# A decoder step on one core: the experts' first gathers and gate splits moved into the attention phase, first rows in halves, a wait moved, and the sample's attention in another order

## The reference, cut to what matters

```python
x = x + MemoryCrossAttn(RMSNorm(x))   # 4 heads over 256 memory tokens
x = x + HierMoE(RMSNorm(x))           # top-1 of 4 groups, then top-2 of 8 experts in it
...
def memory_attn(hn, mem_k, mem_v, w_mq, w_mo):
    q = (hn @ w_mq).reshape(B, T, MEM_HEADS, MEM_DH)
    s = jnp.einsum('bthd,bmhd->bhtm', q, mem_k) * (MEM_DH ** -0.5)
    p = jax.nn.softmax(s, axis=-1)
    return jnp.einsum('bhtm,bmhd->bthd', p, mem_v).reshape(B, T, -1) @ w_mo
...
def expert_block(args):
    xblk, e = args
    h = jax.nn.silu(xblk @ w_e_gate[e]) * (xblk @ w_e_up[e])
    return h @ w_e_down[e]
```

## Time and profile before

| | |
|---|---|
| median of 3 runs | 1961.62 us (1959.93 to 1963.73) |
| profiled execution, its own time | 1965.48 us |
| its span in the trace | 1963.7 us |
| PE busy | 1794.7 us, 91% of the span |
| DVE busy | 1184.4 us, 60% |
| ACT busy | 823.7 us, 42% |
| attention phase ends, experts' phase begins | about 1314.5 us into the span |

### The profile page before, as it was taken

The page is one execution under the profiler, slowest core; times in us unless marked ns, Lnnn a source line. Parts: engine busy times, 40 slices in busy tenths (PEclk is TensorE's granted clock), DMA queues, the critical chain, the costliest instruction groups (busy, mean ns, idle before and its releaser), DMA issues. The chain is left out here.

```text
span 1963.7 us, 35654 instructions
## 1 busy us (share of the span) xinstructions
PE 1794.7 (91%) x14904; PEld 1478.9 (75%) x14904; DVE 1184.4 (60%) x1339; ACT 823.7 (42%) x940; POOL 341.7 (17%) x308
## 2 busy tenths in 40 slices
PE   7999998988888885889999999868999999999995
PEld 6998886777777764678788888647888888878882
DVE  4543111667777665641433433368898898898885
ACT  5111211333343321520212121127777777778763
POOL 1322001233344322000000000011111111111105
PEclk9999998899999987899999999878999999999997
DMA  7756335023222204755200101959999999999988
GB/s 290 243 180 204 115 96 180 13 75 110 97 85 75 85 15 129 258 207 202 97 33 33 65 33 43 371 207 355 403 404 402 404 403 401 403 402 400 405 331 284
DMA packets 113062, 419.13 MB, mean 213 GB/s; under 512 B 26852, under 2 KB 45352, under 8 KB 84008
## 3 DMA queue, kind: packets, MB, share of 16 engines
q1 hardware_dynamic: 100680, 373.76, 51.2%
q0 software_dynamic: 7072, 25.69, 3.5%
q10 hardware_dynamic: 5184, 17.82, 2.2%
HBM read 350.26 MB, written 75.36 MB: 217 GB/s over the span
## 5 line engine op out<-in xcount | busy, mean ns | idle before, releaser
L2715 DVE TENSOR_TENSOR ex_wd_lo<-ex_raw,ex_wd_hi 128x2048 fp32r<-128x2048 f32 x62 | 141.8, 2289 | 50.6 <-ACT ex_wd_hi L2889 50.6
L2715 DVE TENSOR_TENSOR ex_wg_lo<-ex_raw,ex_wg_hi 128x2048 fp32r<-128x2048 f32 x66 | 148.4, 2286 | 10.7 <-ACT ex_wg_hi L2889 10.7
L2715 DVE TENSOR_TENSOR ex_wu_lo<-ex_raw,ex_wu_hi 128x2048 fp32r<-128x2048 f32 x64 | 143.7, 2284 | 0.7 <-ACT ex_wu_hi L2889 0.6
L2889 ACT CAST ex_wg_hi<-ex_raw 128x2048 fp32r<-128x2048 f32 x66 | 125.9, 1910 | 31.6 <-PE banks L2604 23.2
L2889 ACT CAST ex_wd_hi<-ex_raw 128x2048 fp32r<-128x2048 f32 x62 | 118.5, 1913 | 44.5 <-PE banks L2604 26.5
L2889 ACT CAST ex_wu_hi<-ex_raw 128x2048 fp32r<-128x2048 f32 x64 | 122.5, 1915 | 32.4 <-PE banks L2604 32.4
L516 PE MATMUL banks<-pj_w_hi,pj_x_hi 128*128 128x448 f32 (+1 forms) x288 | 109.6, 381 | 11.2 <-DVE pj_x_lo L347 11.2
L2604 PE MATMUL banks<-ex_wg_hi,ex_x_hi 128*128 128x512 f32 x256 | 104.8, 409 | 10.5 <-issue 5.4
L516 PE MATMUL banks<-pj_w_lo,pj_x_hi 128*128 128x448 f32 (+1 forms) x288 | 109.4, 380 | 0.0
L2604 PE MATMUL banks<-ex_wu_hi,ex_x_hi 128*128 128x512 f32 x256 | 102.4, 400 | 0.0
L2604 PE MATMUL banks<-ex_wg_lo,ex_x_hi 128*128 128x512 f32 x256 | 101.5, 397 | 0.0
(11 more groups left out here) (462 smaller groups left out, 4566.8 us busy)
## 6 DMA issues: line engine op xcount, KB each, us to landing
ex_raw<-w_e_gate SPq DMA_DIRECT2D x64, 1024.0 KB, 7.7
ex_raw<-w_e_up SPq DMA_DIRECT2D x64, 1024.0 KB, 7.3
ex_raw<-w_e_down SPq DMA_DIRECT2D x64, 1024.0 KB, 7.2
blocks<-ex_y ACTq DMA_DIRECT2D x32, 512.0 KB, 7.6
mx_pin<-proj SPq DMA_DIRECT2D x8, 1664.0 KB, 7.6
h<-at_h SPq DMA_DIRECT2D x18, 512.0 KB, 2.8
at_slots<-cache_mem_k SPq DMA_DIRECT2D x8, 1024.0 KB, 12.9
at_slots<-cache_mem_v SPq DMA_DIRECT2D x8, 1024.0 KB, 11.9
```

Source lines behind the costliest of these rows:

```text
L2715: v.tensor_tensor(w_lo(w), raw[:, j], as_f32(w_hi(w)), ALU.subtract).then_inc(S_("w_split"), 1)
L2889: act.copy(w_hi(home(j, n)), raw[:, j]).then_inc(S_("w_high"), 1)
```

## The change: what it does

In the experts' entry: the first two gathers are issued by POOL at the end of the attention phase, as soon as `slot_tok` is known, on semaphores of their own (`landed`); ACT makes the high parts of the first expert's two gate pieces there too, in a buffer that the two phases share. For this the last `hn` row is made in another way: DVE multiplies the row by the gain (`rows`), ACT scales it. POOL made this product before. In the experts' phase the first rows are turned, cast and subtracted in two halves. In every step PE waits for `gated` of the expert before ahead of its gate pieces, and for `h` behind them; ACT now waits for `h` ahead of `tanh`.

In the samples' attention: keys are issued ahead of five small tables, the second half of the scores goes between the last two parts of `attend(7)`, the softmax of the samples comes ahead of `back_sum(7)`, and the values' first half ahead of the router of tile 7. The router's weights are laid out on the host so that one plain transfer loads them.

```diff
@@ SP, attention
                         sp.wait_ge(S_("queried"), TILES)
+                        for b in range(DB):
+                            sp.dma_start(slots[:, b].rearrange("p m n -> p (m n)"), d["cache_mem_k"][b]).then_inc(S_(f"keys{b}"), 16)
                         for dst, src in ((strict[:], d["upper"]), (cnt_c[:], d["count"]), (valid[:], d["valid"]), (token[:], d["token"]), (fold[:], d["i64"])):
                             sp.dma_start(dst, src).then_inc(S_("tables"), 16)
-                        for b in range(DB):
-                            sp.dma_start(slots[:, b].rearrange("p m n -> p (m n)"), d["cache_mem_k"][b]).then_inc(S_(f"keys{b}"), 16)
...
-                sp.wait_ge(S_("weights"), 16 * len(PIECES))
@@ POOL, attention
-                po.wait_ge(S_("h_normed"), 1)
-                by_row = lambda ap: ap.rearrange("p (q c) -> p q c", c=KC)
-                po.tensor_tensor(hn[:].rearrange("p (c q) -> p q c", c=KC), by_row(rows[:]), by_row(gf[:]), ALU.mult).then_inc(S_("hn_ready"), 1)
+                xg, landed = first_rows
...
+                po.wait_ge(S_("hn_stored"), 16 * TILES)
+                po.wait_ge(S_("slots_known"), 1)
+                for b in range(2):
+                    po.indirect_dma_start(xg[:, b], None, d["hn"], bass.IndirectOffsetOnAxis(ap=slot_tok[:, b:b + 1], axis=0)).then_inc(landed[b], 16)
@@ DVE, attention
                     mean_square(h[:, SB], hn[:], st[:, 29:30], ms_c(1)).then_inc(S_("back_ms"), 1)
+                    v.wait_ge(S_("h2_turned"), 1)
+                    v.tensor_tensor(rows[:], h[:, SB], gf[:], ALU.mult).then_inc(S_("h2_gained"), 1)
...
+                    if i == NT - 1:
+                        maxima(NT, 2, 6)
+                        divide(NT, 2)
                     back_sum(i)
-                back_row(NT - 1)
-                maxima(NT, 2, 6)
-                hn_turned(NT - 1)
-                divide(NT, 2)
-                logits(NT - 1)
                 v.wait_ge(S_("p_turned"), TILES)
                 v.tensor_copy(bT[:, 0:4, :], PS[:, 7, :].rearrange("p (c t) -> p c t", t=P)).then_inc(S_("pT"), 1)
+                back_row(NT - 1)
+                hn_turned(NT - 1)
+                logits(NT - 1)
                 prompt_choices()
@@ ACT, attention
-                act.activation(rows[:], h[:, SB], ACT.Copy, scale=rstd_c(1)).then_inc(S_("h_normed"), 1)
+                act.wait_ge(S_("h2_gained"), 1)
...
+                act.activation(hn[:].rearrange("p (c q) -> p q c", c=KC), by_row(rows[:]), ACT.Copy, scale=rstd_c(1)).then_inc(S_("hn_ready"), 1)
+                act.wait_ge(S_("weights"), 16 * len(PIECES))
+                for j in range(2):
+                    act.copy(gate_hi[:, j], raw[:, j])
@@ PE, experts
-                    pe.wait_ge(S_("x_lo"), n + 1)
+                    if not first:
+                        pe.wait_ge(S_("gated"), n)
+                    for j in (0, 1):
+                        if first and j == 0:
+                            pe.wait_ge(S_("x0_lo"), 1)
+                        else:
+                            pe.wait_ge(S_("x_lo"), n + 1)
+                        gate_up_piece(j, par, count(j))
                     if not first:
                         pe.wait_ge(S_("h"), n)
-                    for j in (0, 1):
-                        gate_up_piece(j, par, count(j))
-                    if not first:
                         turn_h(pe).then_inc(S_("h_turned"), 1)
@@ DVE, experts
                 for j in (0, 1):
                     low(j, j + 1)
-                rows_low(0, 0)
+                for hf in range(2):
+                    v.wait_ge(S_(("x0_hi", "x_hi")[hf]), 1)
+                    cs = slice(hf * KC // 2, (hf + 1) * KC // 2)
+                    v.tensor_tensor(x_lo[:, 0, cs], rows_in()[:, cs], as_f32(x_hi[:, 0, cs]), ALU.subtract).then_inc(S_(("x0_lo", "x_lo")[hf]), 1)
@@ ACT, experts
+                    if not first:
+                        act.wait_ge(S_("h"), n)
                     tanh(n, 2 if first else done_gu(n, 1))
...
-                for j in (0, 1):
-                    high(j, 1)
-                rows_high(0, 0)
+                act.sem_inc(S_("w_high"), 2)
```

More of the change, by code:

```diff
@@ L1595, in _ @@
                         sp.wait_ge(S_("queried"), TILES)
+                        for b in range(DB):
+                            sp.dma_start(slots[:, b].rearrange("p m n -> p (m n)"), d["cache_mem_k"][b]).then_inc(S_(f"keys{b}"), 16)
                         for dst, src in ((strict[:], d["upper"]), (cnt_c[:], d["count"]), (valid[:], d["valid"]), (token[:], d["token"]), (fold[:], d["i64"])):
                             sp.dma_start(dst, src).then_inc(S_("tables"), 16)
-                        for b in range(DB):
-                            sp.dma_start(slots[:, b].rearrange("p m n -> p (m n)"), d["cache_mem_k"][b]).then_inc(S_(f"keys{b}"), 16)
                 sp.wait_ge(S_("routed"), NT)
[L1601 to L1605, removed]
+                sp.dma_start(wr[:], d["w_router"]).then_inc(S_("router_s"), 16)
+                sp.dma_start(gc[:], d["g_ffn_by_row"]).then_inc(S_("router_s"), 16)
                 sp.wait_ge(S_("os_done"), 2)
@@ L2245, in attend @@
                     for j in range(NPC):
-                        if i == NT - 1 and j == 1:
-                            sample_scores(0)
+                        if i == NT - 1 and j % 2 == 1:
+                            sample_scores(j // 2)
                         ins = project(pe, WO, j, 2, o_hi, o_lo if i < NT else None)
@@ L2369, in _ @@
                     attend(i)
-                sample_scores(1)
-                turn_hn(NT - 1)
-                router(NT - 1)
                 pe.wait_ge(S_("p_ready"), TILES)
@@ L2379, in _ @@
                 sample_values(0)
+                turn_hn(NT - 1)
                 turn_outputs(0)
+                router(NT - 1)
                 sample_values(1)
@@ L2424, in phase_experts @@
         NCNT = 2 * NE + NOVER + EPG + 8 + CAP + NBLK
+        sb("xg_home", [P, 2, D])
+        xg, landed = first_rows
         cnt_c, token = sb("cnt", [P, NCNT]), sb("token", [P, TILES])
@@ L2564, in gather @@
                     po.indirect_dma_start(xg[:, bf], None, d["hn"], bass.IndirectOffsetOnAxis(ap=idx[:, bf:bf + 1], axis=0)).then_inc(S_(f"rows{bf}"), 16)
-                for n in range(2):
-                    gather(n, n)
+                po.sem_inc(S_("idx"), 2)
                 with po.Fori(1, NE // 2) as it:
@@ L2628, in turn_x @@
                 def turn_x(it, bf):
-                    pe.wait_ge(S_(f"rows{bf}"), 16 * it + 16)
+                    if isinstance(it, int) and it == 0:
+                        pe.wait_ge(landed[bf], 16)
+                    else:
+                        pe.wait_ge(S_(f"rows{bf}"), 16 * it)
                     turn_rows(pe, bf).then_inc(S_(f"rows_used{bf}"), 1)
@@ L2659, in step @@
                         downs(n - 1, turn_last if final else None)
-                turn_x(0, 0)
+                pe.wait_ge(landed[0], 16)
+                for c in range(KC):
+                    ins = pe.transpose(PS[:, c // 4, c % 4 * P:c % 4 * P + P], xg[:, 0, c * P:(c + 1) * P], ident[:])
+                    if c == KC // 2 - 1:
+                        ins.then_inc(S_("x0_turned"), 1)
+                ins.then_inc(S_("rows_used0"), 1)
                 step(0, 0, 0, first=True)
@@ L2935, in _ @@
                 act.sem_inc(S_("y"), 1)
-                for j in (0, 1):
-                    high(j, 1)
-                rows_high(0, 0)
+                act.sem_inc(S_("w_high"), 2)
+                for hf in range(2):
+                    act.wait_ge(S_(("x0_turned", "rows_used0")[hf]), 1)
+                    cs = slice(hf * KC // 2, (hf + 1) * KC // 2)
+                    act.copy(x_hi[:, 0, cs], rows_in()[:, cs]).then_inc(S_(("x0_hi", "x_hi")[hf]), 1)
                 for j in (2, 3):
@@ L3012, in build @@
             split += [of(n, [P, 2, PW]) for n in ("wg_lo", "wd_hi", "wd_lo")]
-        phase_attention(core, PS, routed, raw)
+            xg = of("xg", [P, 2, D], F32)
+        first = xg, [nc.alloc_semaphore(name=f"first_rows{b}") for b in range(2)]
+        phase_attention(core, PS, routed, raw, split[2], first)
         core.end_phase()
```

24 lines of the change are left out of this document (15 added, 9 removed).

## The result

The changed kernel took 1949.5 us (median of 5 runs, 1943.85 to 1952.61), the kernel before 1961.62 (5 runs, 1959.93 to 1963.73). The ratio is 0.993, with a 95% interval of 0.9915 to 0.9945. The time came out 2.6 us under the forecast of 1952.1 and inside its range. But the traces show that three terms of the sum were wrong, two in one direction and one in the other, so that the closeness of the number is in part luck.

The account below looks back on a forecast made before the run. The prediction took PE to set the pace in the experts' loop, with the transfers close behind. Its terms, +0.15 - 9.5 + 2.4 - 2.5 = -9.45 us, put the median of 1961.6 at 1952.1; the 8-in-10 range was 1945.5 to 1958.

Parts of the forecast that it names:

- Samples' attention: Reordered samples' attention: the last projection starts at about 1287.2 in place of 1289.24, a gain of 2.0 us.
- Samples' choice: Samples' choice of experts: DVE's new product costs 1.25 us, removing POOL's product saves 2.1; net gain 0.85.
- The phase's end: End of the attention phase: POOL's two gather issues and the engines' meeting take 5.5 us, not 2.5; a loss of 3.0.
- rival (d): Phase's end: gathers hold it over 3.9 us, or samples' chain is later; 2 to 4 us more, 1954 to 1956; chance 0.06.
- The entry: Experts' phase, from its begin to the first down product: 34.9 us in place of 44.4, a gain of 9.5.
- The clock: First down product: PE's 2.8 us stand brings one more half-clock start, a charge of 2.4 us, bounds 0 and 2.4.
- The loop: Experts' loop: PE's 13 waits for the hidden row, 2.5 us in all, go; a gain of 2.5.
- Rival (e): Experts' loop: transfers can't follow PE's 405 GB/s and steps grow, so the kernel is slower; at 394 GB/s 1965; chance 0.03.

Follow-up runs that it names:

- one_early: The changed kernel with only the first gather ahead of the phase's end, the second at the next phase's start; 1950.6 us (1 run).
- busy_queue: The changed kernel with two added 2 MB copies between scratch tensors, issued by SyncE once the table of slots is known; 1956.2 us (1 run).
- wait_alone: The kernel before with only the moved wait for the hidden rows, and ScalarE's wait ahead of its tanh; 1947.9 us, ratio 0.9918 to before.
- order_wait: The kernel before with the other order of the samples' attention and the moved wait, without the entry's gathers, casts and halves; 1953.4 us, ratio 0.9952.
- first_high2: gathers_first with ScalarE's high half of the first up piece moved ahead of the rows' casts; 1945.4 us, ratio 0.9918 to before.
- gathers_late: The changed kernel with both first gathers moved back to the start of the experts' phase; 1947.2 us, ratio 0.9913 to before.
- gathers_first: gathers_late with one added wait on VectorE for the gathers' issue, ahead of its first low halves; 1946.7 us, ratio 0.9915 to before.
- product_later: The changed kernel with VectorE's new product with the gain put behind the samples' logits; 1949.6 us, ratio 0.993 to before.
- wait_half: The changed kernel with PE's wait for the hidden rows put between a step's two gate pieces; 1948.7 us, ratio 0.9925 to before.

## Why the prediction was right, step by step

The time fell inside the range, and the moved wait did remove both waits that the prediction named, the one at the entry and the one in the loop. That it fell so near the forecast is in part luck: the loop gave 8.0 us more than its term and a charge of 2.4 did not come, while the phase's end cost 3.8 us more than its term and the part behind the loop grew. The gain also lies elsewhere: the prediction had 9.5 us of it in the entry and 2.5 in the loop, and the moved wait alone, with 4.7 and 10.3 there, makes the kernel as fast as the whole change does.

- **Samples' attention (-2.0):** right in kind, too large. The last projection starts at 1286.30, which is 1.3 us earlier once 1.6 are taken off. The first values started at 1263.77 and waited for the transfer of the values rather than for the probabilities' copy, and the second group took 5.08 us, at half clock at first (0.50 over 1276 to 1278), where I had counted on the full one.
- **Samples' choice (-0.85):** -1.2. The small instruction takes 0.23 us instead of 2.29, and the root 1.46 instead of 0.54: it starts at 1299.29 beside VectorE's product and ends 0.41 us behind it. Here GpSimd is the one that waits, which no row of before had shown. The Trainium skill (SBUF — State Buffer, section "SBUF: two separate sides") says that of a VectorE instruction with two SBUF inputs and a GpSimd one that reads SBUF the one that starts second waits for the whole instruction of the first; the trace agrees. Not foreseen: ScalarE's write of the row in a strided order takes 2.04 us, the contiguous one 1.15; no run changes that order alone.
- **The phase's end (+3.0): failed.** It measured +6.8 (9.48 less 2.66). I counted the issues on GpSimd, 3.9 us, and the meeting; one_early and busy_queue show that the landing counts, 4.8 us and more behind the last issue. The 3.8 us more are inside the 2 to 4 us of rival (d), to which I gave 0.06; its time of 1954 to 1956 did not come, because the loop gave more than that.
- **The entry (-9.5):** -9.55, from T to the first down product 34.82 us (1352.04 - 1317.22) against a forecast of 34.9, with the first weight product at T + 5.4. The long stand did become one of 2.95 us in front of the down product, where 2.8 were forecast. By wait_alone about half of this term, 4.7 us, belongs to the moved wait; the other 5.0 (T to first weight product, 10.4 to 5.4) belong to gathers, casts and halves together (the casts and the halves were not taken apart), and are paid for with the 6.8 of the phase's end.
- **The clock (+2.4):** did not come in the changed kernel; it did in order_wait and first_high2 after a stand of the same length. I had bounds of 0 and 2.4 and took the wrong end; the same stand gives either.
- **The loop (-2.5): failed.** It measured -10.5. The step was "PE waited for the hidden row 13 times, 2.5 us in all". The mechanism was right, the wait goes; its size was read from booked idle time, where the period of the steps, 18.14 and 18.35 against 17.88, has it whole.
- **Rival (e)**, slower by the transfers: refuted. With six pieces, a gather and a store each 17.88 us (7.3 MB) the loop asked for some 410 GB/s and moved 411, and PE had no gap in it.

Up to the last down product the forecast had -9.45 and the marks show -15.7: 8.0 from the loop and 2.4 from the clock in one direction, 3.8 from the phase's end and 0.35 net from the samples' part in the other. Of these 6.3 us beyond the forecast the medians show only 2.6: the tail grew by 2.5, which takes as much off, the profiled executions stood 3.9 and 1.2 us above their medians, which takes off another 2.7, and the earlier phases were 1.6 faster, which adds to it.

## What to carry to other kernels

Price a wait in a loop by the distance between starts, step against step, and not by the idle time booked before an instruction: here a quarter of it was booked. A transfer issued by GpSimd ahead of a point where the engines meet is not free even if nobody waits for it, since the meeting does; issue it just behind the meeting, and keep large VectorE instructions off its issue. When a bundle of edits has one result, take out each part once: one moved wait was the whole gain here.

## What the hardware did that I had not expected

- The meeting of the engines waits for the landing of GpSimd's gathers (the next transfer comes 1.5 us behind it) and not for SyncE's copies in flight.
- GpSimd's gather issue takes 1.21 us alone, and 2.84 beside VectorE's subtractions of 2.29 us each; in the loop it ends 0.83 us behind the subtraction that it met.
- A stand of 2.94 to 2.96 us of PE before the first down product left the clock at 1.00 in six profiled executions (the changed kernel, wait_alone, gathers_late, gathers_first, product_later, busy_queue) and was followed by half clock in two (order_wait, first_high2).
- Behind the last down product PE stands 14.3 to 19.7 us for nothing that the profile names, in executions whose code there is alike (`wait_half` and `product_later` 19.7, `gathers_late` and the kernel before 14.3, the changed kernel 17.6). The stand grew by 3.3 us from before to changed, which is more than the 2.5 us that the tail grew. Its cause was not tried and stays open.
